# Two token blocks of attention queries turned by small transfers and VectorE block transposes in place of TensorE transposes

## The reference

```python
proj = h @ w_in                                     # h = rms_norm(x, norm_mix)
rq, rk, rv, rg, dq, dk, dvv = jnp.split(proj, cuts, axis=-1)
dq = rms_norm(dq.reshape(b, s, 4, 2, 64), diff_q_norm)   # norm over 64 features
dk = rms_norm(dk.reshape(b, s, 4, 2, 64), diff_k_norm)
sc = einsum('bqhmd,bkhmd->bhmqk', dq, dk) * 64 ** -0.5   # ALiBi and causal mask follow
p = softmax(sc);  a = p[:, :, 0] - lam * p[:, :, 1]
out = einsum('bhqk,bkhe->bqhe', a, v)
```

## Time and profile before

| | |
|---|---|
| median of 3 runs | 975.06 us (974.97 to 976.45) |
| the profiled execution, its own time | 975.14 us |
| its span (first to last instruction) | 973.2 us |
| TensorE busy in the span | 962.9 us, 99% |
| VectorE, ScalarE busy | 684.2 us, 499.4 us |
| granted clock of TensorE, mean | 0.998 of full speed |

### The profile page before, as it was taken

One profiled execution on the slowest core, in us unless ns is written; L12 is line 12 of the kernel. 1 busy time (PEld: TensorE's weight loads), 2 busy tenths in 40 slices (PEclk: granted clock), 3 DMA queues, 4 the chain that ended last, 5 costly groups with the idle time before them and its releaser, 6 DMA issues.

```text
span 973.2 us, 13269 instructions
## 1 busy us (share of the span) xinstructions
PE 962.9 (99%) x5190; PEld 830.0 (85%) x5190; DVE 684.2 (70%) x716; ACT 499.4 (51%) x680; POOL 18.8 (2%) x20
## 2 busy tenths in 40 slices
PE   8999999999999999999999999999999999999997
PEld 8988888888888888888888888899888888888886
DVE  4679758857676767876767676585764577777676
ACT  5454676663434344834343446574866554343433
POOL 0001000030000000000000000000000000000000
PEclk9999999999999999999999999999999999999999
DMA  7855496654565555655555554634444545656551
GB/s 239 280 173 174 149 284 196 234 176 159 187 207 181 200 186 175 192 186 185 197 182 185 187 197 134 220 123 174 167 136 152 160 143 173 215 172 215 172 173 43
DMA packets 126754, 177.23 MB, mean 182 GB/s; under 512 B 12714, under 2 KB 95100, under 8 KB 126588
## 3 DMA queue, kind: packets, MB, share of 16 engines
q1 hardware_dynamic: 125996, 174.28, 54.1%
q10 hardware_dynamic: 720, 2.43, 0.6%
HBM read 175.65 MB, written 1.05 MB: 182 GB/s over the span
## 4 chain that ended last, share of the span: by engine, by line
PE 95%; DVE 2%; ACT 1%; issue 1%; DMA 1%; ACTq 0%; DVEq 0%
PE up_banks L699 12%; PE gate_banks L699 12%; PE bank L470 9%; PE bank L471 9%; PE bank L472 9%; PE up_banks L470 7%; PE up_banks L472 7%; PE up_banks L471 7%; PE up_banks L704 6%; PE gate_banks L704 6%; PE up_banks L563 2%; PE up_banks L566 1%; PE bank L621 1%; PE bank L638 1%; DMA first_rows<-in_norm_mix_pre 1%
## 5 line engine op out<-in xcount | busy, mean ns | idle before, releaser
L1691 DVE TENSOR_TENSOR w_lo<-stage,w_hi 128x2048 fp32r<-128x2048 f32 x81 | 185.5, 2290 | 96.5 <-ACT w_hi L1140 96.5
L1685 DVE TENSOR_TENSOR w_lo<-stage,w_hi 128x2048 fp32r<-128x2048 f32 x78 | 178.3, 2289 | 74.5 <-ACT w_hi L1133 74.3
L1133 ACT ACTIVATE w_hi<-stage 128x2048 fp32r<-128x2048 f32 x79 | 150.9, 1912 | 66.7 <-PE up_banks L566 20.6
L1140 ACT ACTIVATE w_hi<-stage 128x2048 fp32r<-128x2048 f32 x81 | 152.8, 1904 | 0.0
L699 PE MATMUL gate_banks<-act_both,w_hi 128*128 128x512 f32 x528 | 135.5, 393 | 0.0
L699 PE MATMUL up_banks<-act_both,w_hi 128*128 128x512 f32 x528 | 131.7, 392 | 0.0
L699 PEld LDWEIGHTS up_banks<-act_both,w_hi 128*128 128x128 f32 x528 | 96.7, 188 | 18.4
L699 PEld LDWEIGHTS gate_banks<-act_both,w_hi 128*128 128x128 f32 x528 | 93.9, 189 | 15.8
L1215 ACT ACTIVATE ffn_hi<-gate 128x512 fp32r<-128x512 f32 x30 | 18.9, 631 | 155.7 <-DVE gate L1821 155.7
L470 PE MATMUL bank<-w_hi,ffn_hi 128*128 128x512 f32 x240 | 94.0, 392 | 0.2 <-DVE ffn_lo L1823 0.2
L471 PE MATMUL bank<-w_lo,ffn_hi 128*128 128x512 f32 x240 | 93.8, 391 | 0.0
(11 more groups left out here) (370 smaller groups left out, 1480.0 us busy)
## 6 DMA issues: line engine op xcount, KB each, us to landing
stage<-in_ffn_w SPq DMA_DIRECT2D x66, 1024.0 KB, 5.3
stage<-in_w_in SPq DMA_DIRECT2D x33, 1024.0 KB, 5.3
stage<-in_w_gate_up SPq DMA_DIRECT2D x22, 1024.0 KB, 5.1
stage<-in_w_down SPq DMA_DIRECT2D x11, 1024.0 KB, 4.9
stage<-in_w_out SPq DMA_DIRECT2D x8, 1024.0 KB, 5.5
stage<-in_mem_w_kv SPq DMA_DIRECT2D x8, 1024.0 KB, 5.1
stage<-in_w_branch SPq DMA_DIRECT2D x4, 1024.0 KB, 5.3
stage<-in_mem_w_q SPq DMA_DIRECT2D x4, 1024.0 KB, 5.1
```

The source lines that it names most:

```text
L1133: act.activation(w_hi[:, place, :], stage[:, place, :], copy).then_inc(hi_done, 1)
L1140: act.activation(w_hi[:, place, :], stage[:, place, :], copy).then_inc(hi_done, 1)
L1685: dve.tensor_tensor(w_lo[:, place, :], stage[:, place, :], w_hi[:, place, :].bitcast(F32), ALU.subtract).then_inc(lo_done, 1)
L1691: dve.tensor_tensor(w_lo[:, place, :], stage[:, place, :], w_hi[:, place, :].bitcast(F32), ALU.subtract).then_inc(lo_done, 1)
```

## The change

The eight TensorE transposes of the queries, their two evictions by ScalarE and two turns of the shared bank are removed. Instead SP issues, behind the transfer of chunk 108 (RQ), 32 transfers within the core's own memory: each takes 32 tokens (partitions) by 4 heads by 32 features of `raw_dq` and lays them on 32 partitions of `dq_blocks`, a half of `q_pad` that is free then. VectorE waits for all 32 and turns the 32 by 32 blocks with two transposes into `q_T`; TensorE waits for these before the first logits. As `q_T` is no longer scaled on its way, the queries' weights are multiplied into the keys' weights, once, early in the kernel.

```diff
-A_DQ = [3, 4]
-A_DK = [5, 6]
-A_BEFORE_FFN = [3, 3, 7]
+A_DK = [3, 4]
+A_BEFORE_FFN = [3, 3, 5]
...
+        dq_blocks = q_pad[:, 1, :, :]
...
+            def diff_query_blocks():
+                for tb in range(8):
+                    if tb % 4 == 0:
+                        wait_read(sp, DQ + tb // 4)
+                    for g in range(4):
+                        r = slice(32 * g, 32 * g + 32)
+                        sp.dma_start(dq_blocks[r, :, 32 * tb:32 * tb + 32],
+                                     raw_dq[tb // 4][32 * (tb % 4):32 * (tb % 4) + 32, :].rearrange("i (h f) -> i h f", h=4)[:, :, r]
+                                     ).then_inc(dq_landed, 16)
...
-                    wholes(c, w_in2, col, 2)
+                    for i in range(2):
+                        whole(c + i, w_in2, col + 256 * i, slot(c + i))
+                        if c + i == RQ:
+                            diff_query_blocks()
...
-            def turn_diff_queries(t):
-                wait_read(pe, DQ + t)
-                aux(A_DQ[t])
-                for h in range(4):
-                    mm = pe.transpose(quad[AUX][:, h, :], raw_dq[t][:, h * P:h * P + P], ident)
-                mm.then_inc(aux_done, 1)
...
-            turn_diff_queries(0)
             up_tok(DK, act_hi, act_lo, 1)
-            turn_diff_queries(1)
...
             pe.wait_ge(aux_free, A_DK[0] + 1)
+            pe.wait_ge(dq_turned, 2)
...
-            def diff_queries(t):
-                act.wait_ge(aux_done, A_DQ[t] + 1)
-                act.activation(q_T[:, :, t * P:t * P + P], quad[AUX], copy, scale=par[:, DQN:DQN + 1]).then_inc(aux_free, 1)
...
-            diff_queries(0)
             hi(107)
             diff_key_in(0)
             diff_key_in(1)
-            diff_queries(1)
...
+            then(dve.tensor_tensor(par[:, DKN:DKN + 1], par[:, DKN:DKN + 1], par[:, DQN:DQN + 1], ALU.mult))
...
             dve.reciprocal(diff_f, diff_f).then_inc(diff_f_done, 1)
+            dve.wait_ge(dq_landed, 16 * 32)
+            for i in range(2):
+                dve.transpose(q_T[:, 2 * i:2 * i + 2, :].rearrange("p a t -> p (a t)"),
+                              dq_blocks[:, 2 * i:2 * i + 2, :].rearrange("p a t -> p (a t)")).then_inc(dq_turned, 1)
             lo(108)
             lo(109)
```

More of the change, by code:

```diff
@@ L226, in build @@
         x_landed = sem("x_landed")
+        dq_landed, dq_turned = sem("dq_landed"), sem("dq_turned")
         const_landed, par_landed = sem("const_landed"), sem("par_landed")
```

## The result

| | before | changed |
|---|---|---|
| median of 5 runs | 974.97 us (973.65 to 976.45) | 980.83 us (978.52 to 981.98) |
| ratio, 95% interval | | 1.006 (1.0049 to 1.0072) |
| the profiled execution, span | 973.2 us | 980.2 us |
| from the issue of chunk 108 to the end of the span | 361.4 us | 368.4 us |

The change costs 5.9 us, 0.6%. The forecast of 974.2 was wrong, and the measured time lies above its range; rival 1 had named 979.6 to 980.7. In it the profiled execution lost 7.0 us.

A forecast was written before the change was run, and what follows sets the result against it. TensorE, busy 962.9 of 973.2 us, was taken to bound the kernel. Removing 0.88 us of transposes, with everything added hidden, gave 975.14 - 0.88 = 974.26 us profiled, 974.2 for the median; range 973.6 to 979.0.

The forecast's parts named there:

- rival 1: SP's queue becomes the bound: at 0.65 us per issue chunk 109 lands late, 979.6 to 980.7 us; chance 0.19.
- What is removed: Twice four query transposes on TensorE's chain, 2 x 0.44 = 0.88 us; the ScalarE evictions and bank turns worth nothing.
- The VectorE transposes and the product of the weights: Added VectorE work: two transposes, 1.34 us, ahead of `lo(108)`, and one 0.15 us product near 62 us; all hidden.
- p: Time of one of the 32 issues on SP: 0.47 us, bounds 0.37 to 0.65.
- S: How much later than before ScalarE's `hi(109)` starts; forecast -0.4 us, the gain shrinking from 0.06 us.
- o: Delay at the start of the 32 issues on SP, behind chunk 108: 0.8 us, between 0 and 1.5.
- Landing of chunk 109: Time from this weight chunk's issue on SP to its landing: 5.4 us, so landed at 633.4 us.
- Who waits for chunk 109: A later `hi(109)` on ScalarE moves VectorE's chain down to `lo(111)` equally, then TensorE's product at 658.27 us.
- The room: Slack between the end of `lo(111)` at 657.33 us and TensorE's product at 658.27 us: 0.94 us.
- The sum: TensorE's net shift, the larger of -0.88 us and chunk 109's lateness less 0.94 us: -0.88 us, the whole gain.
- Rival 3: TensorE waits for the new transposes before the logits: +1.4 us at 0.65 us per issue; by late landings 977.5, chance 0.04.
- Rival 4: The removed TensorE transposes cost more than the chain shows, 2.2 us: 972.9 us; chance 0.03 with any other gain.

The follow-up runs named there:

- experiment 1: Changed kernel without its 32 transfers and the wait for them (queries wrong): 972.85 us against 973.90 for the kernel before, ratio 0.9987.
- experiment 2: Changed kernel with only 16 of the 32 transfers (half of the queries wrong): 973.73 us, ratio 0.9994 to the kernel before.
- experiment 4: Changed kernel with the same 32 transfers issued from GpSimd's queue instead of SP's: 973.98 us against 973.90 for the kernel before, ratio 0.9991.
- experiment 6: Changed kernel with chunk 109 issued behind the first 16 transfers and `lo(108)` ahead of VectorE's wait: 976.82 us, ratio 1.0023.
- experiment 5: Changed kernel with one head per transfer, 32 pieces instead of 128 (three of four heads' queries wrong): 979.51 us, ratio 1.0046.
- experiment 10: Changed kernel with 32 transfers of 32 partitions x 1 piece of 128 bytes from HBM (queries wrong): 973.10 us, one execution.
- experiment 8: Changed kernel with 8 transfers of 128 partitions x 4 pieces instead of 32 of 32 x 4 (queries wrong): 974.54 us, ratio 1.0000.
- experiment 12: Changed kernel with 24 of the 32 transfers, one feature group left out (its queries wrong): 974.96 us, ratio 0.9997.
- experiment 3: Changed kernel with `lo(108)` ahead of VectorE's wait for the transfers instead of behind it: 981.00 us, ratio 1.0070.
- experiment 9: Changed kernel with 32 transfers within the core's memory of 32 partitions x 1 piece of 512 bytes (queries wrong): 979.57 us, one execution.

## Why the forecast was wrong

**What is removed:** right, 0.88 us forecast, 0.9 to 1.0 measured (experiments 1, 2, 4).

**The VectorE transposes and the product of the weights:** right. 1.30 us for the two transposes, hidden in experiments 1, 2 and 4; no cost in experiment 1. (In experiment 6 they come late, because the last transfer does.)

**p, the price of an issue: the step that failed.** "The new ones have 128 pieces, so the nearest row is the norm's: p = 0.47." Measured 0.64. I took the number of pieces for what sets the price and picked the row that was nearest in that. The 0.65 us of the memory's transfers, 256 pieces from HBM, seemed an upper bound with pieces to spare; in fact the new transfers have another price, which the trace of before did not contain, and it lay by chance next to that bound. With p = 0.64 and the rest of the forecast as it stood, S is 5.1 and the median 979.2, already above the range. From HBM the number of pieces does count (0.46 us for 32, 0.65 for 256); within the core's memory 32, 128 and 512 pieces cost 0.63, 0.64 and 0.69.

**o:** 0.8 forecast; the first transfer took 0.66 us, so the forecast's reason, the weight chunk ahead, did not act. One transfer took 1.0 us more than the others, but in the middle of the row. In the changed kernel and in experiments 5, 6 and 10 it falls in the same 2 us as one packet of a queue for instructions (0.02 MB); in experiment 8 no such packet stands beside it. So its cause stays open, and that the size came out near 0.8 is luck.

**Landing of chunk 109:** 5.4 forecast, 5.36 measured. 32p + o came to 21.7, where 15.8 was forecast, and S to 5.5 (`hi(109)` began 27.5 us after chunk 108's issue, before 22.0).

**Who waits for chunk 109:** right as a path, with the wrong end. "TensorE took up its product at 658.27. The room is 0.94 us." I had counted to the end of `lo(111)`. RK + 1 also waits for its bank, which the scaling of RQ + 1 empties 0.6 us later. The line stood in VectorE's timeline of before:

```profile
657.25 0.68 DVE L1752 TENSOR_TENSOR gate<-up_banks,rs 128x512 f32<-128x512 f32 x1
```

It ends at 657.93, and in the changed kernel the product follows such an end by 0.14 us: that leaves 0.2 us, not 0.94. These 0.2 us go too once TensorE waits at all, since its first product then takes 0.36 us instead of 0.16. Experiments 10 and 12 agree: at S = -0.5 the end comes 0.5 us earlier, at S = 0 it stands where it stood before, within 0.1 us. So between -0.9 and 0 the gain is as large as chunk 109 is early, and any lateness is loss. Even with p = 0.47 and the rest as forecast (S = -0.4) the gain would have been about 0.4 us, by this working.

**The sum:** the forecast had -0.9 us for the profiled execution, measured were +7.0. Of the 7.9 us between them some 5.4 come from p (with o), 0.9 from the room and 1.5 from the clock, by this working.

**Rival 1** was the truth, with a chance of 0.19. Its working at p = 0.65 gave +4.5 to +5.6; S with the true room gives +5.5, and the fall of the clock, which no part of the forecast foresaw, adds 1.5 in the profiled execution. That its upper figure, 980.7, lies beside the measured 980.8 is partly luck: it has 1.5 for o and 5.8 for the landing, neither of which was measured, where it lacks 0.9 of the room and the clock. **Rival 3** was right that TensorE would wait for the transposes at this p (1.2 us) and that rival 1 hides it (experiment 3); take rival 1 away and it shows (experiment 6). **Rival 4** would have gained 2.2 us; experiments 1, 2 and 4 gained 0.9 to 1.0 from chunk 108 on, which excludes it.

**The range** ended at p = 0.63 on the wrong room and without the clock. The upper values that the forecast itself named (0.65 for p, 1.5 for o, 5.8 for the landing) would have carried it to 980.7.

**The page on descriptors** (the Trainium skill, DMA: Bandwidth & Descriptors, "Anatomy of one DMA") is written for GpSimd's path, and the rows are SP's. That many can be emitted before it shows agrees with the transfers within the core's memory, where 32 and 512 pieces differ by 0.06 us an issue, and less with those from HBM, where 32 and 256 differ by 0.19. The forecast took its p from the rows, and what it missed was not the pieces but the price with few of them, 0.63 us.

## What to carry to other kernels

A queue that feeds a ring of buffers has a budget: before putting n issues into it, multiply n by the dearest issue in the trace, the more so if the trace has no transfer of the new kind, and ask how early the next feed must be out; here 16 fitted with room, 24 used up the gain, and 32 cost some seven times what they were to bring. Put such transfers on a queue that is idle, or between the feeds rather than in a block. And when the room of a late chunk is read off, go through every wait of the instruction at its end: the bank it writes as well as the weights it reads.

## What the runs showed of the hardware

- Back to back on SP, transfers of 32 partitions took 0.63 us each from within the core's memory and 0.46 us from HBM, with the same 32 pieces of 128 bytes (experiments 5 and 10); pieces of 512 bytes did not change the former (experiment 9). From GpSimd's queue the transfers of 32 x 4 pieces came every 0.55 us (experiment 4), from SP's every 0.64.
- A VectorE block transpose of 128 x 512 float32 takes 0.67 to 0.71 us. Half of the 32 transfers of the changed kernel landed within 1.9 us of their issue, the slowest in 5.1 us.
- Ahead of RK + 1 TensorE stood for 2.2 us in the changed kernel and in experiments 3, 5 and 9. In or behind this hole the granted clock went from 2.4 to 1.2 GHz in the first three, for 3.4 us in the changed kernel (1.5 us lost) and over 662 to 666 us at least in experiment 5, and stayed at 2.4 GHz in experiment 9. This may be one source of the 3.5 us between the runs of the changed kernel; with a profile of one of them alone it is not shown.
